# GpSimd's sums of weights, begun after the second unit of the last stage in place of the sixteenth

## The chip, the core and the metric

The kernel runs on one core of a Trainium2 chip. The core has five engines with queues of their own: TensorE (PE in the profile: matmuls, and PEld for its weight loads), VectorE (DVE), ScalarE (ACT), GpSimd (POOL) and SyncE (SP), which here only issues DMAs. GpSimd issues DMAs too, from its own queue. Sixteen DMA engines carry all of them. The metric is the device time of one execution in microseconds, the median of several runs.

## The reference

One layer of a streaming encoder over 2048 prompt frames and 32 sample frames, width 1024:

```
u = rms_norm(h);  q, k, v, a, b = split(u @ w_in)          # 8 heads of 64; conv of 512 channels
att = softmax(q k^T / 8 + rel_bias, own chunk and 8 before) v
cv  = silu(layer_norm(causal_conv31(a * sigmoid(b)) + conv_b))
h   = h + concat(att, cv) @ w_out
u   = rms_norm(h);  gate, up = split(u @ w_gate_up)         # 2 x 2816 columns
h   = h + (silu(gate) * up) @ w_down
y   = h + sigmoid(rms_norm(h) @ w_ple_gate) * (p @ w_ple_proj)
```

It also returns the newest keys, values and convolution inputs. All data is float32.

## The kernel before

The 2080 frames are five blocks of 416 columns; a product is of 128x128 weight tiles with 128x416 activations. For precision each float32 operand is split into a high part, which TensorE takes as it is, and a low part (the value less its high part); each tile product is three matmuls (high x high, high x low, low x high: `passes`, L193 to L198).

There are three stages, `project`, `attend` and `finish`. The change is in the last one. `finish` walks over a list of *units*, numbered v from 0; U0 is what the semaphore `used` counts when the stage begins, and TensorE raises it by one after each unit. A unit is one or two 128-row outputs of one weight matrix: kinds X and Y (w_out, attention half and convolution half, four units each in block 0), G and U (gate and up columns, 11 of each per half), D (w_down, 8 per half) and P (w_ple). Units 0 to 7 are X and Y of block 0, and unit 8 is its first G. The matmuls of unit 0 are issued at the end of `attend`. Most units in this stretch have 24 matmuls.

Around each unit (the numbers of buffers in brackets):

- SyncE loads the raw weights of unit v + 4 (`weights`, L2610) into one of two buffers (`x` in the trace), after the unit that held it was split. In block 0 it also stores the low parts (`low_store`, L2616) for the later blocks, which only reload them.
- ScalarE makes the high part (`high`, L2708, two buffers), VectorE the low part (`weight_low`, L2831, block 0 only, four buffers). TensorE waits for the low part.
- VectorE and ScalarE take the results out of PSUM, form squares, sigmoids and the hidden tiles (L2895 to L3024), and run the depthwise convolution of a later block in small rounds (`taps`, L2878). At the opening of the stage they also have the last steps of block 0's convolution (L2846 to L2862).

Blocks 0 to 2 are done this way. Blocks 3 and 4 are done together by `last_pair`, which saves matmuls with sums of weight tiles, as in Strassen's scheme. These sums are made by GpSimd while `finish` works on blocks 0 to 2: `weight_sums` (L1664 to L1698). It has 60 rounds (`SUMS`) with one buffer (a part of `c_top`) and no overlap between rounds: two loads of 256 KB (L1687), four additions and subtractions of 128x256 (L1689 to L1695), one store of 512 KB to the scratch tensor `w_gu_sums` (L1698). Each round waits for the store before it, and for the count `sums_after` of `used`. In `last_pair` ScalarE waits once for the last store (L1971), ahead of its fourth piece of weights (L1651), and SyncE waits for the rounds of a piece that reads them (L1876). GpSimd's only later work is L2268.

Of the kernel before, what the change touches and what calls it, by code (L numbers as in the profile page):

```python
# [17 lines left out]
KD = D // P  # L18
# [6 lines left out]
KF = FF // P  # L25
# [16 lines left out]
SINGLE, FIRST, SECOND = 3, 4, 3  # L42
# [5 lines left out]
def build(nc, t):  # L48
# [3 lines left out]
    with ExitStack() as ctx:  # L52
# [36 lines left out]
        with ExitStack() as middle:  # L89
            c["rstd"] = sb("rstd", [P, NB, N], until=middle)  # L90
            for n in ("q_in0", "q_in1", "q_in2", "q_in3", *(f"kv_in{g}" for g in range(8)), "first_g", "bias_in0", "first_z"):
# [4 lines left out]
            attend(nc, t, c, s, {"w_in": each, "hi_done": QKV + 6, "lo_done": QKV + 6, "used": NB * QKV + 4})  # L96
        GLUS = 8 * (NB - 1) + 2
        finish(nc, t, c, s, {"w_in": each + 16 * GLUS // 2, "hi_done": QKV + 6 + GLUS, "lo_done": QKV + 14,
                             "used": NB * QKV + 6 + GLUS, "low_dma": [16 * GLUS // 2] * 2 + [0] * 2})

# [2309 lines left out]
def finish(nc, t, c, s, base):  # L2410
# [6 lines left out]
    NTAP = CT * TAPS  # L2417
# [21 lines left out]
    at, count, newest, turn = {}, 0, {}, 0  # L2439
# [42 lines left out]
    with ExitStack() as ctx:  # L2482
        def sem(name):
            return ctx.enter_context(nc.semaphore("c_" + name))
# [27 lines left out]
        W0, H0, L0, U0 = base["w_in"], base["hi_done"], base["lo_done"], base["used"]  # L2512
# [9 lines left out]
        tap = sem("tap")  # L2522
# [54 lines left out]
        def late(u):  # L2577
# [10 lines left out]
            "raw": [top[:, 16 * N + e * KH * P:16 * N + (e + 1) * KH * P] for e in range(3)],  # L2588
            "hi": [flat[:, e * KH * P:(e + 1) * KH * P] for e in range(4)],
            "lo": [flat[:, (4 + e) * KH * P:(5 + e) * KH * P] for e in range(4)],  # L2590
            "newest": newest, "left0": count, "sig0": SINGLE * (KF + KD), "tap": tap, "taps": 4 * NTAP, "sums_after": U0 + 16,
            "mix_staged": MIX0 + 32,
            "pa_at": {down_b + r: k for k, r in enumerate((4, 5, 7, 8, 10, 11, 13, 14))},
            "left": left, "sig_out": sig_out, "gs_out": gs_out, "hid_out": hid_out, "hid_hi": hid_hi, "hid_lo": hid_lo,
# [612 lines left out]
```

## Time and profile before

| | |
|---|---|
| median of 3 runs | 2627.03 us (2625.26 to 2628.12) |
| profiled execution, its own time | 2624.12 us |
| its span | 2622.3 us |
| TensorE busy | 2602.2 us, 99%, 14408 matmuls |
| VectorE busy | 1803.4 us, 69% |
| ScalarE busy | 1222.0 us, 47% |
| GpSimd busy | 467.1 us, 18% |
| DMA | 675.05 MB, mean 257 GB/s |

Matmuls are pipelined: a matmul's modelled time is longer than the distance between the starts of two of them, so that short waits don't show as idle time and the number of matmuls in a stretch says more. A line of the profile names a source line of the kernel, engine and operation, what is written and read, and how long. Idle time before an instruction is put down to what ended it.

### The profile page before, as it was taken

To read this page: it belongs to the slowest core of one execution; us is meant where nothing else is said; L and a number is where in the kernel's file an instruction comes from. 1 tells how busy PE (TensorE), PEld (TensorE's weight loads), DVE (VectorE), ACT (ScalarE), POOL (GpSimd) and SP (SyncE) were. 2 spreads that over 40 slices of the span, in tenths; PEclk is the share of its full clock that TensorE was granted. 3 is DMA by queue.
4 is the path that set the end of the run, shared out by engine and by line. 5 is a ranking of instruction groups with operands and counts; after the bars stand their busy time and mean duration, and the time that the engine had idled before them with its cause. 6 is when DMAs were issued, how large, how long until landed. Compare 5 with 4: busy or idle time off the path is not lost.

```text
span 2622.3 us, 40458 instructions
## 1 busy us (share of the span) xinstructions
PE 2602.2 (99%) x14408; PEld 2542.2 (97%) x14408; DVE 1803.4 (69%) x3303; ACT 1222.0 (47%) x2240; POOL 467.1 (18%) x513
## 2 busy tenths in 40 slices
PE   9999999999999999999999999999999999999999
PEld 8999999999999999999999999999998999999999
DVE  4555478988978878777756876888548655665462
ACT  5444367877764323443334443323435443443453
POOL 6222200000001323223323323333300000000000
PEclk9999999999999999999999999999999999999999
DMA  5666798888677998898888898889895554555677
GB/s 202 213 219 233 252 356 272 266 279 267 205 236 245 296 305 281 294 345 291 319 310 313 283 322 302 318 312 317 299 317 165 169 169 153 174 162 167 196 240 236
DMA packets 316115, 675.05 MB, mean 257 GB/s; under 512 B 36589, under 2 KB 172653, under 8 KB 315373
## 3 DMA queue, kind: packets, MB, share of 16 engines
q1 hardware_dynamic: 297676, 609.55, 70.0%
q0 software_dynamic: 18240, 62.93, 6.8%
q8 instruction: 116, 1.90, 0.3%
q14 instruction: 83, 0.67, 0.1%
HBM read 514.28 MB, written 160.10 MB: 257 GB/s over the span
## 4 chain that ended last, share of the span: by engine, by line
PE 86%; DVE 7%; DMA 4%; issue 2%; ACT 2%; SPq 0%; DVEq 0%; ACTq 0%
PE psum L198 53%; PE psum L2285 23%; PE psum L1509 3%; PE psum L1485 2%; DMA x<-in_w_gu 2%; DVE y L2878 1%; PE psum L1473 1%; PE psum L1472 1%; DVE wres L2831 1%; ACT wres L2708 1%; DMA o_y<-c_top 0%; DVE wres L2087 0%; DVE plain L2078 0%; DMA a_cr<-in_cache 0%; PE psum L837 0%
## 5 line engine op out<-in xcount | busy, mean ns | idle before, releaser
L198 PE MATMUL psum<-uh,wres 128*128 128x416 f32 x3936 | 1118.2, 355 | 5.7 <-DVE wres L2831 2.4
L198 PEld LDWEIGHTS psum<-uh,wres 128*128 128x128 f32 x3936 | 736.6, 188 | 19.2 <-DVE wres L2831 5.3
L198 PE MATMUL psum<-ul,wres 128*128 128x416 f32 x1968 | 687.7, 349 | 0.0
L2708 ACT ACTIVATE wres<-x 128x1024 fp32r<-128x1024 f32 (+2 forms) x234 | 268.5, 1148 | 641.2 <-PE psum L198 533.1
L198 PE MATMUL psum<-wres 128*128 128x416 f32 x2304 | 447.7, 352 | 1.9 <-DVE wres L2831 1.6
L198 PEld LDWEIGHTS psum<-wres 128*128 128x128 f32 x2304 | 430.3, 188 | 9.3 <-issue 2.4
L2285 PE MATMUL psum<-wres 128*128 128x416 f32 x2056 | 418.7, 352 | 4.3 <-issue 1.4
L2285 PEld LDWEIGHTS psum<-wres 128*128 128x128 f32 x2056 | 383.2, 188 | 13.8 <-issue 5.6
L198 PEld LDWEIGHTS psum<-ul,wres 128*128 128x128 f32 x1968 | 370.3, 188 | 6.5 <-issue 1.4
L2878 DVE SCALAR_TENSOR_TENSOR y<-c_top,vec,y 128x416 f32<-128x416 f32 (+1 forms) x600 | 340.2, 634 | 0.8
L1651 ACT ACTIVATE wres<-c_top 128x512 fp32r<-128x512 f32 (+1 forms) x306 | 184.0, 603 | 190.1 <-PE psum L2285 48.2
L1687 POOL DMA_DIRECT2D c_top<-in_w_gu x88 | 62.3, 713 | 746.5 <-PE psum L198 517.4
L2285 PE MATMUL psum<-uh,wres 128*128 128x416 f32 x480 | 137.8, 352 | 0.0
L2285 PE MATMUL psum<-c_hx,wres 128*128 128x416 f32 x640 | 137.5, 351 | 0.2 <-ACT wres L1651 0.2
L1368 ACT ACTIVATE wres<-psum 128x384 fp32r<-128x384 f32 (+5 forms) x256 | 91.0, 405 | 89.3 <-PE psum L1485 88.8
L1239 DVE TENSOR_TENSOR wres<-psum,wres 128x384 fp32r<-128x384 f32 (+5 forms) x256 | 111.0, 441 | 16.7 <-ACT wres L1368 16.5
L2285 PEld LDWEIGHTS psum<-c_hx,wres 128*128 128x128 f32 x640 | 119.5, 188 | 2.2 <-ACT wres L1651 0.5
L2831 DVE TENSOR_TENSOR wres<-x,wres 128x1024 fp32r<-128x1024 f32 (+2 forms) x74 | 99.8, 1348 | 27.5 <-ACT wres L2708 27.5
L1689 POOL TENSOR_TENSOR c_top<-c_top 128x256 f32<-128x256 f32 x60 | 51.2, 853 | 341.4 <-DMA c_top<-in_w_gu 264.7
L1358 ACT ACTIVATE b_pr<-b_pr,b_nmx 128x640 f32<-128x640 f32 (+5 forms) x136 | 103.5, 761 | 4.1 <-DVE b_nmx L1218 4.1
L1509 PE MATMUL psum<-wres 128*128 128x256 f32 (+1 forms) x672 | 98.9, 280 | 0.0
L2285 PEld LDWEIGHTS psum<-uh,wres 128*128 128x128 f32 x480 | 89.7, 188 | 0.8 <-issue 0.2
(277 smaller groups left out, 3448.5 us busy)
## 6 DMA issues: line engine op xcount, KB each, us to landing
x<-in_w_gu SPq DMA_DIRECT2D x132, 512.0 KB, 5.4
wres<-w_gu_lo SPq DMA_DIRECT2D x88, 512.0 KB, 6.2
x<-in_w_down SPq DMA_DIRECT2D x48, 704.0 KB, 5.9
w_gu_sums<-c_top POOLq DMA_DIRECT2D x60, 512.0 KB, 6.0
c_top<-w_gu_sums SPq DMA_DIRECT2D x120, 256.0 KB, 3.0
w_gu_lo<-wres SPq DMA_DIRECT2D x44, 512.0 KB, 6.5
c_top<-in_w_gu POOLq DMA_DIRECT2D x88, 256.0 KB, 5.9
wres<-w_down_lo SPq DMA_DIRECT2D x32, 704.0 KB, 7.0
```

The costliest lines, as they stand in the source:

```text
L198: mm = nc.tensor.matmul(out, w[wp](kw), u[up](ku), start=first and n == 0 and j == 0, stop=last and n == len(kts) - 1 and j == 2)
L1239: last = nc.vector.tensor_tensor(dst(ptl), src, dst(pth).bitcast(F32), ALU.subtract)
L1358: nc.scalar.activation(pr[0:mq, q, 0:w], pr[0:mq, q, 0:w], ACT.Exp, scale=-1.0, bias=nmx[0:mq, q:q + 1], accum_out=rsum[0:mq, q:q + 1]).th ...
L1368: last = nc.scalar.activation(dst(pth), src, ACT.Copy)
L1485: mm = nc.tensor.transpose(ps_t[0:wd, part, at * P:at * P + mq], pr[0:mq, i % 3, k * P:k * P + wd], c["ident"][0:mq, 0:mq])
L1509: mm = nc.tensor.matmul(ps_o[:, q, q0:q0 + nq], rows, pt[0:wd, q, a, q0:q0 + nq], start=x == 0 and j == 0, stop=x == count - 1 and j == 1)
L1651: nc.scalar.activation(f["hi"][n % 4][:, cols], f["raw"][q][:, cols], ACT.Copy).then_inc(c["hi_done"], 1)
L1687: nc.gpsimd.dma_start(v[:, 2 * x:2 * x + 2, :], src).then_inc(moved, 16)
L2285: mm = nc.tensor.matmul(out, w[wp](k), r[rp], start=first and k == 0 and wp == rp == 0, stop=last and k == len(rights) - 1 and wp == 1, sk ...
L2708: nc.scalar.activation(whi[v % 2][:, 0:kts, :], raw[v % 2][:, 0:kts, :], ACT.Copy).then_inc(hi_done, 1)
L2831: nc.vector.tensor_tensor(wlo[v % 4][:, 0:kts, :], raw[v % 2][:, 0:kts, :], whi[v % 2][:, 0:kts, :].bitcast(F32), ALU.subtract).then_inc(l ...
L2878: last = nc.vector.scalar_tensor_tensor(y[:, ct, to], gw[:, ct, fro], vec[:, w:w + 1], y[:, ct, to], ALU.mult, ALU.add)
```

## The change

GpSimd's rounds wait for the end of unit 1 instead of unit 15. What is summed, the order, the buffer and every wait between rounds stay.

```diff
--- before.py
+++ after.py
@@ -2588,7 +2588,7 @@
-            "newest": newest, "left0": count, "sig0": SINGLE * (KF + KD), "tap": tap, "taps": 4 * NTAP, "sums_after": U0 + 16,
+            "newest": newest, "left0": count, "sig0": SINGLE * (KF + KD), "tap": tap, "taps": 4 * NTAP, "sums_after": U0 + 2,
```

The wait stands in `weight_sums`:

```python
        for n in range(SUMS):
            pool.wait_ge(c["used"], f["sums_after"])
            if n:
                pool.wait_ge(moved, sums_stored(n - 1))
```

## Rows read from the trace of the kernel before

**Rows 1.** The page: busy time of the engines, and 40 slices of the span.

```profile
PE 2602.2 (99%) x14408; PEld 2542.2 (97%) x14408; DVE 1803.4 (69%) x3303; ACT 1222.0 (47%) x2240; POOL 467.1 (18%) x513
...
PEclk9999999999999999999999999999999999999999
```

**Rows 2.** POOL's work in order of time and its stores as a group: start, duration, [idle before].

```profile
825.37 1.59 POOL L1687 DMA_DIRECT2D c_top<-in_w_gu  x2 [488.18 <-PE psum L198]
834.48 0.73 POOL L1689 TENSOR_TENSOR c_top<-c_top 128x256 f32<-128x256 f32 x1 [7.52 <-DMA c_top<-in_w_gu]
...
L1698 POOL DMA_DIRECT2D w_gu_sums<-c_top x60: 774/774/791, 839.3 to 1895.5; - x60
```

**Rows 3.** ACT in order of time, its first piece behind the wait for the sums.

```profile
1950.88 0.63 ACT L1651 ACTIVATE wres<-c_top 128x512 fp32r<-128x512 f32 x1 [0.49 <-DMA c_top<-in_w_out]
```

**Rows 4.** The chain that ended last, 740 to 940 us: start, duration, what.

```profile
767.86 6.17 DMA x<-in_w_out
...
775.14 1.23 DVE wres L2831
776.39 6.56 DMA x<-in_w_gu
...
811.17 127.25 PE psum L198 x672
```

**Rows 5.** PE and DVE in order of time, 750 to 812 us.

```profile
751.59 28.67 PE L198 MATMUL psum<-wres 128*128 128x416 f32 x148
...
792.40 0.46 PE L198 MATMUL psum<-uh,wres 128*128 128x416 f32 x1 [0.17 <-DVE wres L2831]
...
811.17 0.46 PE L198 MATMUL psum<-uh,wres 128*128 128x416 f32 x1 [0.35 <-DVE wres L2831]
...
772.74 1.09 DVE L2950 TENSOR_TENSOR z<-psum,z 128x416 f32<-128x416 f32 x2 [2.38 <-PE psum L198]
```

**Rows 6.** Windows: length, then busy us and count per engine, PE clock, DMA share, GB/s.

```profile
775.00:780.00 5.00, 5.00 (x28) 1.00 1.05 408
...
760.00:765.00 5.00, 5.00 (x29) 1.00 0.71 233
...
755.00:790.00 35.00, 35.00 (x185) 34.19 (x184) 28.19 (x46) 21.39 (x32) 0.00 (x0) 1.00 0.94 331
...
940.00:1042.00 102.00, 99.55 (x520) 96.37 (x518) 84.89 (x117) 32.40 (x42) 33.07 (x37) 1.00 0.87 282
1042.00:1830.00 788.00, 784.55 (x4132) 772.47 (x4133) 587.32 (x976) 303.34 (x385) 254.07 (x312) 1.00 0.89 310
1830.00:1900.00 70.00, 70.00 (x368) 68.45 (x367) 34.78 (x48) 30.04 (x40) 20.95 (x30) 1.00 0.87 299
...
785.00:811.00 26.00, 25.43 (x129) 23.47 (x128) 23.98 (x35) 14.04 (x20) 0.00 (x0) 1.00 0.69 211
```

**Rows 7.** DVE, then POOL, in order of time around POOL's first round.

```profile
825.79 0.59 DVE L2981 TENSOR_TENSOR c_top<-c_top 128x416 f32<-128x416 f32 x1
826.30 1.22 DVE L2831 TENSOR_TENSOR wres<-x,wres 128x1024 fp32r<-128x1024 f32 x1
827.43 2.33 DVE L2878 SCALAR_TENSOR_TENSOR y<-c_top,vec,y 128x416 f32<-128x416 f32 x4
...
834.85 0.81 DVE L2981 TENSOR_TENSOR c_top<-c_top 128x416 f32<-128x416 f32 x1
835.70 1.64 DVE L2831 TENSOR_TENSOR wres<-x,wres 128x1024 fp32r<-128x1024 f32 x1
837.27 3.29 DVE L2878 SCALAR_TENSOR_TENSOR y<-c_top,vec,y 128x416 f32<-128x416 f32 x4
...
836.34 1.60 POOL L1693 TENSOR_TENSOR c_top<-c_top 128x256 f32<-128x256 f32 x1
```

**Rows 8.** The chain, 940 to 1042 us: its longest load; then PE in order of time.

```profile
997.03 8.94 DMA x<-in_w_gu
...
1042.93 1.41 PE L198 MATMUL psum<-wres 128*128 128x416 f32 x6 [1.56 <-DVE wres L2831]
```

## The prediction

> **What bounds the kernel now.** I read the views from the coarse to the fine. The page comes first [rows 1]: TensorE (PE) is busy for 99% of the span and its granted clock is full in all 40 slices, VectorE (DVE) has 69%, GpSimd (POOL) 18%. So the time is PE's work plus the moments at which PE is made to wait; an edit that touches no PE instruction can only create or remove such moments. "Busy" hides small ones, since a matmul's modelled time (350 ns) is longer than the distance between two (127.25 us for 672, 0.189 us each [rows 4]), so I also count matmuls per stretch.
>
> Second, POOL's own view [rows 2]. Its sums are 60 rounds: two loads of 256 KB, four additions, one store of 512 KB. The first round's loads start at 825.37 us, after 488 us in which POOL had nothing, and the first and last store are issued at 839.3 and 1895.5: (1895.5 - 839.3)/59 = 17.9 us a round. What reads the sums comes later. ScalarE waits for all of them once, ahead of its fourth piece of weights for the last two blocks; that piece runs at 1950.88, after a wait of 0.49 us for its own load and none for the sums; the last store was issued at 1895.5 [rows 2, 3]. SyncE reads sums only after that. The end of the sums has some 50 us of slack, so ending earlier is worth nothing in itself.
>
> Third, the chain of waits between 752 and 811 us, the start of the last stage [rows 4]. Here the chain isn't PE. It goes through DVE (the convolution's tail and the low parts of the weights), then a weight load of 6.17 us, ScalarE, DVE, another weight load of 6.56 us, ScalarE, DVE again, and comes back to PE at 792.40; from 797.3 to 811.1 it is DVE and ScalarE once more. Only from 811.17 on does it read "PE, 127.25 us, 672 matmuls". PE waits there before 792.40 and 811.17 [rows 5]. The windows show how little room the stretch has [rows 6]: the DMA engines are busy 94% of 755 to 790 us, and DVE 24.0 of the 26 us from 785 to 811.
>
> **The change, part by part.** POOL waits for U0+16 before each round; now for U0+2. The later rounds had this count behind them anyway, so only the first moves. When is the second unit over? PE's row of 148 matmuls starts at 751.59; the first 12 end unit 0, the next 24 are unit 1, so at 28.67/148 = 0.194 us each U0+2 comes at 751.59 + 36 x 0.194 = 758.6 us. The sums start 825.4 - 758.6 = 66.8 us, or 66.8/17.9 = 3.7 rounds, earlier, and end at about 1830. Nothing is added or removed: 60 rounds, 180 DMAs from POOL's queue, 240 additions. POOL has no other work between, and SyncE's queue isn't passed or reordered.
>
> Step 1, **DMA traffic at the start**. Round 1 has its loads in 759 to 768 us (the first ones before took 834.48 - 825.37 = 9.1 us), its store from about 772, and round 2's loads from about 778 [rows 2]. Each of these three moves 0.52 MB; at 408 GB/s, the most that a 5 us window showed there [rows 6], that is 1.28 us of all engines, 3.9 us together. The free share of the windows 760 to 785 is 0.29 x 5 = 1.5 us and sits at 760 to 765, so 0 to 3.9 - 1.5 = 2.4 us falls on the two weight loads of the chain. Both lie on it, with 0.8 us of slack in front of PE's next unit: the low part of unit 6's weights is ready at 775.14 + 1.23 = 776.4 [rows 5] and PE comes to unit 6 at 751.59 + 132 x 0.194 = 777.2. The middle of 0 to 2.4 is 1.2 us; I take **+1.2 us** (0 to 2.4).
>
> Step 2, **additions beside DVE**. The row that shows the price is the first round of before, 834.5 to 839.0 [rows 7]. DVE's operations beside it took 0.81, 1.64 and 3.29 us; the same ones without POOL 0.59, 1.22 and 2.33 [rows 7]. That is 0.22 + 0.42 + 0.96 = 1.6 us a round. The additions of POOL's round 1 (768 to 772) meet DVE waiting for PE and a load, as it idles 2.38 us before 772.74 [rows 5]: 0. Round 2's additions (about 787) and round 3's (about 805) meet the chain where it is DVE. Part of the chain there is ScalarE, PE, and fixed gaps, so half of 1.6 us reaches PE each time: **+1.6 us** (0 to 3.2). Round 4's come at about 823, when the chain is PE again; the very first round of before, at 834 to 839, fell into the same run of PE, and it has no break there [rows 4, 7]: 0.
>
> At this point a rule of the Trainium skill can be set beside the row. The measured operations were stretched by a third, which looks like sharing. The Trainium skill ("SBUF — State Buffer", section "Who interferes with whom") says that VectorE with two inputs in SBUF contends with a GpSimd operation that reads SBUF, and that the loser is blocked outright for the whole instruction. Were every addition of a round (0.73 us undisturbed in its row) to block DVE in full, a round would cost 4 x 0.73 = 2.9 us instead of 1.6 us. The trace has 1.6 us, because POOL is the loser part of the time: its third addition there took 1.60 us [rows 7].
>
> Step 3, **what is taken away at the end**. Four rounds vanish from 1830 to 1900 us. PE has 368 matmuls in those 70 us, 0.190 us each, and no idle time [rows 6]: 0. DVE is at half load there, so the cover is large.
>
> Step 4, **the rounds between**. From 825 to 1830 POOL still does a round each 18 us, with another phase. PE's idle time there is 2.45 us in 940 to 1042 and 3.45 us in 1042 to 1830 [rows 6]; one wait of 1.56 us, at 1042.93, is the largest part [rows 8]. A new phase can remove or double such waits: 0, from -2 to +2 us.
>
> Sum: 1.2 + 1.6 + 0 + 0 = **+2.8 us**. A later PE start at 811 is never made good, since from there PE runs without a pause. The profiled execution took 2624.12 us (span 2622.3 and 1.8 us around it), so it would become 2626.9. It is 2.9 us below the median of the runs shown, 2627.03; on that median the forecast is 2629.8 us. A measurement of this kernel can tell about 0.2%, 5.3 us, from no change, so the forecast is "the same", leaning slow.
>
> **The rivals.**
>
> A, *hidden altogether*: -1 to +1 us, 2627. For it: the chain has PE waits of under a microsecond only, and weights are prepared one to two units ahead. Against: the chain passes through DMA and DVE for 40 us without PE.
>
> B, *the opening falls behind*: slower than I say. Both terms come at their upper end, with 2.9 us a round: that is what the skill's rule of full blocking would give here, in rounds 2, 3 and 4. By the rows: all of the 3.9 us of DMA and four rounds at 1.6 us = 3.9 + 6.4 = 10.3 us at most, half of it 5.2; 2632 to 2637. It decides from the point at which DVE, whose idle time is 26 - 24.0 = 2.0 us in 785 to 811 [rows 6], can no longer make up 1.6 us per round before the next one, 18 us later, so that PE waits at each unit from 792 to about 850. Against: from 811 to 938 six rounds ran beside a DVE with much the same work, and PE had no pause [rows 4].
>
> C, *faster*: the new phase clears the stretch 940 to 1042. The chain there holds weight loads of up to 8.9 us [rows 8] against 6.2 and 6.6 us at the opening [rows 4], and PE has 520 matmuls instead of 102/0.189 = 539 [rows 6]. The 19 missing ones are 3.6 us, and the PE idle of 1042 to 1830 is 3.45 us more. If most of it went and the opening cost nothing, the gain is 5 to 7 us: 2621. It needs both, and rounds stay as frequent there as before.
>
> D, *the start doesn't move*: would POOL be held by something else than the count? It has only this wait and an empty queue before it. Its effect would be that of A.
>
> **Chances.** Forecast (+1 to +5 us) 0.55; A with D 0.23; B 0.17 (0.13 of it above +5.3 us); C 0.05 (0.02 beyond -5.3 us). So faster 0.02, same 0.85, slower 0.13. Range: the forecast's own bounds are 0 and 2.4 + 3.2 = 5.6 us, and -2 to +2 for the phases and about 1.5 us for the spread of the three runs; together 2626 to 2634, which leaves out 1 in 10 on either side.
>
> **What the next profile would show.** POOL's first load at 758 to 759 us and its last store near 1829. In the opening: the weight loads of the chain above 6.6 us, DVE's 128x1024 subtraction at 1.6 us in place of 1.22 beside POOL's second and third round, and the unbroken run of PE starting 2 to 4 us after 811.2. In 1830 to 1900 the same 368 matmuls. Step 1 is wrong if those loads stay at 6.2 to 6.6 us; step 2 if PE's waits in 780 to 811 don't grow while DVE's rows do; step 3 if PE gains matmuls at the end. The prediction fails on the slow side if PE waits at each unit up to 850, on the fast side if 940 to 1042 has its full 539 matmuls.

## The result and the profile after

The change makes the kernel slower. In six runs beside six of the kernel before, the median is 2634.6 us against 2626.15 us, +8.45 us; the ratio is 1.0029, with a 95% interval of 1.0018 to 1.0039. Ten more runs of the same kernel, the experiment `e11_change_again` below, gave 1.0023 (1.0013 to 1.0033). The forecast was +2.8 us, "the same, leaning slow", with a range of 2626 to 2634 us: the sign was right and the size too small; the first measurement lies just above the range, and the +6.0 us of the second would lie inside it. The ratios, here and below, leave out three far slower executions (2852, 4279 and 6625 us), which the medians include.

The page of the changed kernel differs little from that of the kernel before [rows 1]: TensorE is busy 3.2 us longer and the span is 9.1 us longer.

```profile
PE 2605.4 (99%) x14408; PEld 2545.4 (97%) x14408; DVE 1803.3 (69%) x3303; ACT 1222.7 (46%) x2240; POOL 472.2 (18%) x513
```

2.4 of the 9.1 us lie before the changed place: the last group of matmuls ahead of the stage's stream starts at 751.52 us in this trace and at 749.12 in that of the kernel before. Over all the traces here that moment lies between 749.1 and 753.3, without any edit ahead of it. So from here on I count from the opening, T0, the first matmul of this group (L1572).

GpSimd starts as forecast, after unit 1. Its work in order of time, and its stores as a group (compare [rows 2]):

```profile
761.59 1.59 POOL L1687 DMA_DIRECT2D c_top<-in_w_gu  x2 [423.60 <-PE psum L198]
767.96 0.73 POOL L1689 TENSOR_TENSOR c_top<-c_top 128x256 f32<-128x256 f32 x1 [4.78 <-DMA c_top<-in_w_gu]
...
L1698 POOL DMA_DIRECT2D w_gu_sums<-c_top x60: 777/777/793, 772.5 to 1856.2; - x60
```

The chain that ended last, 755 to 905 us (compare [rows 4]). The two weight loads of the opening take 7.38 and 8.66 us, and the chain then stays with loads and VectorE; the long run of TensorE, from 811 us before, comes only behind 902 us.

```profile
770.62 7.38 DMA x<-in_w_out
...
780.37 8.66 DMA x<-in_w_gu
...
834.34 7.21 DMA x<-in_w_gu
...
845.99 9.37 PE psum L198 x48
...
866.99 7.91 DMA x<-in_w_gu
```

TensorE in order of time. In the kernel before there were only short waits here, 0.17 to 0.35 us [rows 5]; now there is a long one at 791.79, and there are more behind 811:

```profile
791.79 0.48 PE L198 MATMUL psum<-uh,wres 128*128 128x416 f32 x1 [2.04 <-DVE wres L2831]
...
814.86 0.45 PE L198 MATMUL psum<-uh,wres 128*128 128x416 f32 x1 [1.13 <-DVE wres L2831]
821.15 0.46 PE L198 MATMUL psum<-uh,wres 128*128 128x416 f32 x1 [1.49 <-DVE wres L2831]
...
845.99 0.46 PE L198 MATMUL psum<-uh,wres 128*128 128x416 f32 x1 [1.44 <-DVE wres L2831]
```

Behind the wait of 2.04 us TensorE's clock is at its lower level, 1.2 in place of 2.4 GHz, for some 3.4 us. The windows below (length, TensorE busy and count, granted clock, DMA share, GB/s) have a granted clock of 0.50. Their counts include matmuls that run across a window's ends; a window of 1 us at full clock counts 7. By the starts, 14 matmuls take 4.30 us from 791.79 on, where 14 x 0.189 = 2.65 us were enough: about 1.7 us are lost on top of the wait.

```profile
791.00:792.00 1.00, 0.21 (x1) 1.00 0.09 35
792.00:793.00 1.00, 1.00 (x4) 0.54 0.16 23
793.00:794.00 1.00, 1.00 (x4) 0.50 0.75 188
794.00:795.00 1.00, 1.00 (x5) 0.50 0.84 225
795.00:796.00 1.00, 1.00 (x6) 0.76 1.04 418
```

A cost of another kind: GpSimd's third round of additions meets the first step of the convolution, a tensor_scalar of VectorE with one large input. Its four take 3.46 us; in the kernel before they took 1.71 us. GpSimd isn't slowed at all there. VectorE in order of time in the kernel before, then VectorE and GpSimd after:

```profile
800.79 1.71 DVE L2888 TENSOR_SCALAR y<-c_top,vec 128x416 f32<-128x416 f32 x4
```

```profile
809.01 3.46 DVE L2888 TENSOR_SCALAR y<-c_top,vec 128x416 f32<-128x416 f32 x4
...
809.02 0.73 POOL L1689 TENSOR_TENSOR c_top<-c_top 128x256 f32<-128x256 f32 x1 [8.18 <-DMA c_top<-in_w_gu]
809.82 0.76 POOL L1691 TENSOR_TENSOR c_top<-c_top 128x256 f32<-128x256 f32 x1
```

The windows that answer to [rows 6]: the loss is in the opening. 785 to 811 us has 111 matmuls instead of 129, and 1830 to 1900 has the same 368. In between, 940 to 1830 us has 30 matmuls more than before, of which more below.

```profile
755.00:790.00 35.00, 34.02 (x178) 32.66 (x176) 25.76 (x36) 17.21 (x25) 8.63 (x11) 1.00 0.98 350
785.00:811.00 26.00, 23.54 (x111) 21.37 (x110) 20.74 (x26) 14.48 (x19) 8.03 (x10) 0.93 0.76 259
940.00:1042.00 102.00, 100.70 (x531) 98.69 (x530) 86.13 (x118) 31.34 (x39) 33.46 (x36) 1.00 0.89 290
1042.00:1830.00 788.00, 787.26 (x4151) 775.96 (x4150) 586.77 (x977) 303.02 (x386) 245.48 (x302) 1.00 0.88 310
1830.00:1900.00 70.00, 70.00 (x368) 68.46 (x367) 35.77 (x51) 31.19 (x41) 9.02 (x12) 1.00 0.73 259
```

### The profile page after: what moved, and what is told of

It is laid out like the page before. It is cut to its first block, busy times and chain, and to the rows that moved or that the text cites. A ratio compares the mean times of both kernels' runs of the same rounds, so it can differ in the third digit from the quotient of the medians.

```text
span 2631.4 us, 40458 instructions
## 1 busy us (share of the span) xinstructions
PE 2605.4 (99%) x14408; PEld 2545.4 (97%) x14408; DVE 1803.3 (69%) x3303; ACT 1222.7 (46%) x2240; POOL 472.2 (18%) x513
## 4 chain that ended last, share of the span: by engine, by line
PE 86%; DVE 6%; DMA 4%; issue 2%; ACT 1%; SPq 0%; POOL 0%; DVEq 0%; ACTq 0%; POOLq 0%
PE psum L198 53%; PE psum L2285 23%; PE psum L1509 3%; PE psum L1485 2%; DMA x<-in_w_gu 2%; PE psum L1473 1%; DVE wres L2831 1%; PE psum L1472 1%; DVE y L2878 1%; ACT wres L2708 1%; DMA o_y<-c_top 0%; DMA a_room<-in_w_in 0%; DVE wres L2087 0%; DMA a_cr<-in_cache 0%; PE psum L837 0%
```

## The experiments

One number is read from each trace: TensorE's matmuls in the 140 us behind T0, up to about 889 us, where block 0's first D unit begins. These are the windows of the kernel before, its second profile (`e8`), the change, and its second profile (`e11`), in this order:

```profile
749.12:889.12 140.00, 139.25 (x723) 1.00 0.85 274
```

```profile
749.53:889.53 140.00, 137.88 (x713) 1.00 0.83 269
```

```profile
751.52:891.52 140.00, 132.05 (x667) 0.99 0.85 285
```

```profile
750.93:890.93 140.00, 135.64 (x691) 0.99 0.86 287
```

At 0.189 us each, the change is 56 and 32 matmuls behind the first trace, a *lag* of 10.6 and 6.1 us, and the kernel before differs from itself by 10, or 1.9 us. One trace is good to some 2 to 4 us. The totals of the two measurements, +8.45 and +6.0 us, differ by as much.

| kernel | matmuls to T0 + 140 | lag, us | median, before beside it | ratio (95%) |
|---|---|---|---|---|
| before, twice | 723, 713 | 0, 1.9 | | |
| the change | 667 | 10.6 | 2634.6, 2626.15 | 1.0029 (1.0018 to 1.0039) |
| `e11` the change again | 691 | 6.1 | 2634.02, 2628.06 | 1.0023 (1.0013 to 1.0033) |
| `e1` additions cut | 702 | 4.0 | 2628.32, 2626.7 | 1.0004 (0.9995 to 1.0013) |
| `e2` DMAs cut | 699 | 4.5 | 2629.24, 2626.7 | 1.0007 (0.9997 to 1.0017) |
| `e3` both cut | 719 | 0.8 | 2627.6, 2626.7 | 1.0001 (0.9993 to 1.001) |
| `e6` first round only | 712 | 2.1 | 2630.58, 2626.62 | 1.0021 (1.0012 to 1.003) |
| `e4` start after unit 8 | 682 | 7.8 | 2631.49, 2626.7 | 1.0018 (1.0008 to 1.0029) |
| `e12` after unit 11 | 718 | 0.9 | 2628.14, 2628.06 | 1.0006 (0.9994 to 1.0017) |
| `e5` after unit 23 | 722 | 0.2 | 2627.03, 2626.62 | 1.0004 (0.9995 to 1.0013) |
| `e7` pause | 719 | 0.8 | 2626.85, 2626.62 | 1.0008 (0.9995 to 1.0022) |
| `e9` late taps, early sums | 691 | 6.1 | 2635.22, 2628.06 | 1.0031 (1.0019 to 1.0043) |
| `e10` late taps | 721 | 0.4 | 2633.18, 2628.06 | 1.0018 (1.0006 to 1.003) |

### Which part of a round costs: traffic or additions

For `e1_tiny_adds` the first six rounds add 8 of 256 columns (w = 8, q = 256); for `e2_tiny_dmas` they move 8 of 256 columns (w = 256, q = 8), with a memset of the buffer first and the missing stores made up ahead of the last round; for `e3_both_tiny` both are 8. `sums_after` is U0 + 2, and each of the six rounds waits for four more units than the one before. This holds the shortened rounds apart, but the third starts 49 to 52 us behind T0, against 48 in the change, and the fourth 68 to 72 against 65, so the meetings with VectorE aren't exactly those of the change.

```diff
-            pool.wait_ge(c["used"], f["sums_after"])
+            pool.wait_ge(c["used"], f["sums_after"] + 4 * min(n, 5))
+            w, q = (8, 256) if n < 6 else (256, 256)
...
-                nc.gpsimd.dma_start(v[:, 2 * x:2 * x + 2, :], src).then_inc(moved, 16)
+                nc.gpsimd.dma_start(v[:, 2 * x:2 * x + 2, 0:q], src[:, :, 0:q]).then_inc(moved, 16)
...
-            nc.gpsimd.tensor_tensor(a22, a21, a22, ALU.add).then_inc(made, 1)
+            nc.gpsimd.tensor_tensor(a22[:, 0:w], a21[:, 0:w], a22[:, 0:w], ALU.add).then_inc(made, 1)
```

> The sums start after unit 1, as in the change, but in the first six rounds, from 760 to about 860 us, the four additions work on 8 of 256 columns (the sums of these rounds are not those of the reference); all DMAs keep their full size, and round n of the six waits for unit 1 + 4n. The profile of the change shows TensorE 60 matmuls (11.3 us) behind at 940 us. Theory DMA (the traffic of the rounds delays the chain's weight loads): nearly all of the cost stays, 8 us or more of the 11.3 and weight loads of 7 to 9 us at the opening. Theory additions (VectorE is slowed beside GpSimd's additions, and the chain is VectorE's): the cost falls to 3 us or less, and the loads get shorter by themselves as they start earlier. If both share it: 4 to 7 us.

> The counterpart: additions at full size, while the loads and the store of the first six rounds move 8 of 256 columns, 1/32 of the bytes (the missing stores are made up late, before the last round; the sums of these rounds are not those of the reference). Theory DMA: little cost is left at 940 us, 0 to 3 us behind the kernel before. Theory additions: 8 us or more of the 11.3 stay, with VectorE's 128x1024 subtraction at 1.6 us in the opening beside each round. If both share it: 4 to 7 us, and the two experiments add up to about the whole.

> The control: additions and DMAs of the first six rounds are both cut to 8 of 256 columns. Both theories: TensorE is not behind at 940 us (less than 1 us), and the total is that of the kernel before or some us less, since 940 to 1800 us then has the same rounds with another phase, and the last rounds end 60 us earlier. If 4 us or more remain at 940 us, the cost is in something else than bytes and additions: GpSimd's queue, its DMA issues or the semaphores.

Measured: lags of 4.0, 4.5 and 0.8 us. Neither theory holds alone; the cost is shared. With both cut the lag is within the spread of the kernel before, so the queue, the issue of the DMAs and the semaphores cost nothing that shows. 4.0 - 0.8 = 3.2 us are the traffic's alone and 4.5 - 0.8 = 3.7 us the additions'; together with the 0.8 that is 7.7 us, between the change's two traces. Each of these is from one trace and good to some 2 us.

The rows bear the two parts out. The two weight loads of the opening's chain take 8.59 and 7.50 us in `e1` and 5.81 and 6.58 us in `e2`. In `e2` TensorE's clock halves behind a wait of 1.57 us and one of 0.23 us, which costs the same 1.7 us as above; it doesn't in `e1`. So of the 3.7 us some 1.7 are the clock's and some 2.0 are left for waits on VectorE. VectorE comes late there because GpSimd's second round (additions up to 790.2 us) meets four operations on its chain, which take 0.58 to 0.65 us each in the kernel before. VectorE in order of time in `e2_tiny_dmas`:

```profile
786.35 1.13 DVE L2904 SCALAR_TENSOR_TENSOR ul<-z,vec,uh 128x416 fp32r<-128x416 f32 x1
787.40 1.12 DVE L2910 TENSOR_TENSOR c_top<-c_top 128x416 f32<-128x416 f32 x1
788.45 1.12 DVE L2904 SCALAR_TENSOR_TENSOR ul<-z,vec,uh 128x416 fp32r<-128x416 f32 x1
789.49 1.12 DVE L2910 TENSOR_TENSOR c_top<-c_top 128x416 f32<-128x416 f32 x1
```

GpSimd's additions beside them start at 787.10, 788.15 and 789.20 us, the same 1.05 us apart: the two engines go in turns, and both are slowed (the additions take 0.97 us, 0.73 undisturbed).

In the totals the parts are +1.6 and +2.5 us and not clear of zero, while both together, the change, are. Why they don't add up there isn't shown.

### One round alone

```diff
-            pool.wait_ge(c["used"], f["sums_after"])
+            pool.wait_ge(c["used"], f["sums_after"] + 14 * (n > 0))
```

> Only the first round starts after unit 1; the other 59 wait for unit 15 as before. Theory of full DMA engines (755 to 790 us): the first round's loads and store, and its additions beside the weights of units 4 and 5, already cost 3 to 5 us at 940 us, with the chain's two weight loads at 7 us or more. Theory that it is a matter of how long the rounds go on while VectorE is behind: 0 to 1.5 us.

Measured: a lag of 2.1 us, under the 3 to 5 us expected by the one theory and above the other's 1.5. The loads on the chain did lengthen, as step 1 of the forecast has it:

```profile
770.47 7.28 DMA x<-in_w_out
...
780.12 7.60 DMA x<-in_w_gu
```

With 6.17 and 6.56 us before [rows 4] that is 2.15 us more, and 2.1 us arrive. A single load says little, since it spreads without any early round too (5.61 to 7.55 us); the sum of the two is steadier. It is 12.4 to 13.5 us in the eight traces in which both are on the chain and no full-size DMA of a round is beside them, 14.9 us here, and 16.0 to 16.6 us in the four with two rounds of full traffic (the change twice, `e1`, `e9`).

The total is +4.0 us, more than the opening explains. This trace has a wait of 2.46 us at 965 us, and the clock halves behind it; from T0 + 190 to T0 + 290 it has 497 matmuls where the kernel before has 514 and 516, some 3 us. The chain isn't TensorE's there in the kernel before either. Whether the first round has to do with it stays open.

### From which unit on the sums are free

`e4_start9`, `e12_start12` and `e5_start24` are the kernel before with `"sums_after": U0 + 9`, `U0 + 12` and `U0 + 24`.

> The sums start after unit 8 (about 791 us) in place of unit 1 or 15, nothing else changed. Theory DMA (the full DMA engines of 755 to 790 us): most of the cost is avoided, 0 to 3 us behind at 940 us, since only VectorE is full from here on. Theory additions: the rounds still meet VectorE at over 90% in 785 to 820 us, so 4 to 8 us of cost.

> The sums start after unit 11 (about 805 us). Start after unit 8 cost 8.1 us at 140 us after the opening and 4.8 us in total, start after unit 15 nothing. Theory reserve: VectorE makes up its backlog between 791 and 825 us, so the price falls in between, 2 to 5 us at 140 us and 1.5 to 4 us in total. Rival (the price is that of a few coincidences of a round with a critical operation): anything from 0 to 8 us, not in order of the start.

> The sums start after unit 23 (about 861 us), 36 us later than in the kernel before; the last round would end near 1936 us, still ahead of ScalarE's wait near 1950. Theory (the opening's G and U units up to 889 us can't carry rounds because VectorE and the weight loads have no reserve there): in the kernel before, the two rounds at 825 to 861 us fell into a run of TensorE with no break, so nothing or at most 1 us is gained at 940 us. Total: the kernel before, within 2 us. Rival (each round in that stretch costs 2 us or more wherever it falls): 3 to 5 us faster. If the slack at the end was misread: slower, with ScalarE waiting for the sums at 1950 us.

Measured: after unit 8 a lag of 7.8 us, nearly the change's, though its first loads start at 795 us, behind the stretch of full DMA engines. After unit 11 0.9 us, within the spread, and nothing more to gain after unit 23. The price doesn't fall slowly with the start, as the theory of reserve had it for `e12` (2 to 5 us); it stops between units 8 and 11. The chain of `e4_start9` shows what its rounds met:

```profile
804.83 2.98 DVE y L2888 x4
...
820.14 1.77 DVE wres L2831
...
830.17 8.40 DMA x<-in_w_gu
...
841.19 1.76 DVE wres L2831
```

These are the tensor_scalars of the convolution again (2.98 against 1.71 us), two weight subtractions of 1.77 in place of 1.22 us, and a load of 8.40 us. TensorE waits 2.62 us behind the last, and its clock halves again:

```profile
843.00 0.46 PE L198 MATMUL psum<-uh,wres 128*128 128x416 f32 x1 [2.62 <-DVE wres L2831]
```

In `e12_start12` the first load comes behind the tensor_scalars, which keep their 1.71 us. VectorE, then GpSimd:

```profile
803.15 1.71 DVE L2888 TENSOR_SCALAR y<-c_top,vec 128x416 f32<-128x416 f32 x4
...
808.96 1.59 POOL L1687 DMA_DIRECT2D c_top<-in_w_gu  x2 [469.95 <-PE psum L198]
```

The split is the same in the other traces: 2.98 to 3.46 us where full-size additions meet them (the change twice, `e2`, `e4`, `e9`), 1.71 us elsewhere.

`e5_start24` also measures the slack at the end. Its last store is issued at 1946.3 us and ScalarE waits 5.1 us for it:

```profile
ACT wres L1651 <- DMA w_gu_sums<-c_top: 5.1, 1, 5.1
```

In the trace read for the prediction the last store is at 1895.5, so its slack is 1946.3 - 5.1 - 1895.5 = 46 us, near the 50 us read there. That isn't a property of the kernel alone. In the second trace of the kernel before (`e8`) the stores as a group are

```profile
L1698 POOL DMA_DIRECT2D w_gu_sums<-c_top x60: 777/777/793, 839.0 to 1924.7; - x60
```

and leave some 16 us.

### A pause in the second half

```diff
-            pool.wait_ge(c["used"], f["sums_after"])
+            pool.wait_ge(c["used"], f["sums_after"] + 35 * (n >= 7))
```

> The kernel before with a pause: round 7 (959 us in the kernel before) and all after it wait for unit 50 (about 1000 us), so that 959 to 1000 us has no round; the end moves to about 1936 us. TensorE lost 19 matmuls (3.6 us) in 940 to 1042 us in the kernel before, with two or three rounds in the paused part. Theory (rounds cause these waits): 1.5 to 3 us are gained by 1042 us, and the total is 1 to 3 us lower. Rival (the convolution's taps and the weight loads cause them by themselves, or the change's own traces, which lost only half as much there with as many rounds, just had another phase): 0, within 1 us either way.

Measured: 2626.85 against 2626.62 us, ratio 1.0008 (0.9995 to 1.0022). No gain in the total. In the trace, T0 + 190 to T0 + 290 has 529 matmuls where the kernel before has 514 and 516, so 2.5 to 2.8 us are gained in the paused part, as the theory had it; the 50 us ahead of it, with a wait of 1.61 us at 894 us, have ten fewer than the first trace of the kernel before, which takes most of it back. But `e1`, `e4` and `e12` have 523 to 525 there without a pause. What the rounds cost in that stretch isn't settled.

### Is it VectorE's reserve

`e10_late_taps` moves convolution rounds out of the first half's U units, `e9_late_taps_early_sums` does so with U0 + 2.

```diff
-            1: spread(60, places("U", 0) + places("D", 0) + places("U", 0, 1)),
+            1: spread(60, places("D", 0) + places("U", 0, 1)),
```

> The change, and with it the 60 convolution rounds for block 1 are spread over the D units and the second half's U units alone, none over the first half's U units. That takes 2.3 us of VectorE's work out of each pair of G and U units from 800 to 889 us. The change's trace is 10.8 us behind at 140 us after the stage opened (889 us), the kernel before 0 and 1.7 us in its two traces. Theory reserve (after the opening VectorE has nearly no idle time, so that each round's 1.6 us and its later weight loads reach TensorE): the lag at 140 us falls to 3 to 6 us, what the first two rounds and the clock cost. Theory of the weight loads (rounds lengthen them, and the ring of two buffers is too short, whatever VectorE does): it stays at 8 us or more. The total isn't comparable with the kernel before, as the second half gets more work; it is with the next kernel.

> The control of the one before: the convolution rounds moved, the sums after unit 15 as before. Both theories: 0 at 140 us after the opening, within 1 us, since TensorE had no wait there but at the opening; behind by some us at 310 us, where the second half now has three convolution rounds per unit. The total 0 to 10 us above the kernel before. The difference of the two totals is the price of the early start when VectorE has more idle time: 3 to 5 us by the theory of reserve, 8 us by the other.

Measured: 6.1 and 0.4 us of lag. All of `e9`'s waits in the 140 us stand ahead of 797 us, the largest 1.74 us and the next 1.56 with the clock halved behind them; the next one, 1.16 us, comes at 896 us, with rounds 17 to 19 us apart in between. That agrees with reserve. But `e11_change_again`, with the convolution rounds in place, has its last wait of the 140 us at 823.59 and the same lag of 6.1 us. Against that trace nothing was gained, so the experiment doesn't decide. The difference of the totals is 2635.22 - 2633.18 = 2.0 us, less than the change's own 6 to 8, with intervals that overlap.

### The same kernels again

> The kernel before, profiled a second time, to see what two traces of one kernel differ by: the time at which the last stage opens (749 to 753 us in the traces so far), TensorE's count of matmuls at 940 us after the opening (both theories: equal within 1 us), and the count in 940 to 1042 and in the two later places (1580 to 1620, 1740 to 1780 us) where the change's trace gained back 5 us. If this trace also gains there, the 5 us are no effect of the change.

> The change itself a second time. It says how far one trace may be trusted: the lag at 140 us after the opening was 10.8 us. If TensorE's clock falls again after a wait of 2 us or more at the first G unit, that is a part of the change's price; if not, it is an accident of one trace. Total: 7 to 9 us above the kernel before.

Measured: the second trace of the kernel before has one wait more in the 140 us, 1.01 us at 881.5, and 0.79 us at 891.6. So the unbroken run of TensorE from 811 to 938 us was in part luck of the first trace. The second settles another point. The change's first trace seemed to win back some 5 us late, between 940 and 1100 us and around 1600 and 1750 us. In 1560 to 1630 and 1730 to 1800 the first trace of the kernel before has 360 and 365 matmuls, its second one has

```profile
1560.00:1630.00 70.00, 70.00 (x366) 1.00 0.86 300
1730.00:1800.00 70.00, 70.00 (x373) 1.00 0.91 324
```

so those waits were an accident of the trace read for the prediction, and the change gives nothing back there. Over the whole way from T0 + 140 to T0 + 1850 something may come back: its two traces have 8953 and 8949 matmuls, the kernel before 8933 and 8936, which is 2.5 to 3.8 us, and the eight other kernels that leave the convolution rounds in place have 8913 to 8938. The totals, +8.45 and +6.0 us, don't show it.

The change's second trace repeats the opening: loads of 7.24 and 8.78 us, a wait of 2.06 us at the first G unit, and the clock halved behind it.

## Why the prediction fell short, by its steps

**Where the time goes** was right. The loss arises behind T0 and ahead of the first D unit, and 1830 to 1900 us has its 368 matmuls (step 3, 0 us, right). Step 4 took 0 for the rounds between, from -2 to +2 us; the change's traces seem to get 2.5 to 3.8 us back there, if that is more than spread. The start was right within a microsecond once the trace's own 2.4 us are taken off. The last store came at 1856 and not 1829, because a round took 18.4 us and not 17.9; it took 18.4 us in the second trace of the kernel before as well and 18.1 in that of the change, so this is spread and not the change's doing, and it costs nothing.

**Step 1, traffic**, is the term that was most too small. The mechanism was right, with both weight loads on the chain. I took the middle of 0 to 2.4 us, 1.2, by counting free DMA capacity. The two loads together grew by 1.21 + 2.10 = 3.3 us in the change (3.1 us against the mean, 12.9 us, of the eight traces without early traffic), by 2.15 us in `e6` with one round, and the traffic alone cost 3.2 us in `e1`. The bound was wrong as well: bytes at the highest rate, set against the free share, gave at most 2.4 us. Why a load grows by more than that no run shows. The later loads of the change's chain (7.21 and 7.91 us) don't count against it: the second trace of the kernel before has 6.74 and 8.28 us at 846 and 865 us.

**Step 2, additions**: 1.6 us (0 to 3.2) against 3.7 us in `e2`, 2.0 without the clock. So the size was nearly right, and where it arises in part wrong. "Round 1: 0" was wrong: its additions stretch VectorE's work ahead of the first load (in the change the subtraction at 769.01 takes 1.59 us), and TensorE waits 0.51 us at 769.35 in `e2`. "Half reaches TensorE" was too little at round 3: in `e2` the tensor_scalars take 3.41 us, 1.7 more, and the two waits of TensorE behind them are 0.30 and 1.48 us against 0.35 us before, so 1.4 of the 1.7 us arrive. The price was read beside operations with two inputs, and the tensor_scalars lose as much alone, 1.75 us in the change. "Round 4: 0" nearly held: the wait of 1.49 us at 821.15 ends ahead of round 4's first addition at 822.82, and the wait behind that round is 0.17 us (0.18 in `e11`). The 1.44 us at 846 us come behind round 5 and a load of 7.21 us, and only in the first of the change's traces.

**What no step had** is the clock: 1.7 us more behind a wait of about 2 us at the first G unit, in both traces of the change. In `e2` and `e9` it falls near the same place, behind a wait of under 1.6 us with one of 0.23 us close by, in `e4` at 843 us behind 2.62 us, and in the opening of no other kernel here. With 3.2 us of traffic, 2.0 of additions, 1.7 of the clock and the 0.8 that `e3` leaves, the sum is 7.7 us, where the forecast had 1.2 + 1.6 = 2.8.

**The rivals.** B, the opening falls behind, had the price that was measured (2632 to 2637). Its sign, a wait at each unit from 792 to about 850 us, came only in part: the change's first trace has five waits of over 0.2 us there, in some twelve units, and its second trace has two. I gave B 0.17, against it the run of 811 to 938 us; that argument was weak, as the second trace of the kernel before shows. Whether its mechanism, VectorE's missing reserve, is the cause `e9` couldn't decide. The Trainium skill's rule of full blocking ("SBUF — State Buffer", section "Who interferes with whom") stood behind the same rival with 2.9 us a round. The traces have less: single operations grew by up to 0.58 us (the subtraction from 1.22 to 1.59 or 1.77 us, additions from 0.58 to 1.12 or 1.16 us), less than one undisturbed addition of 0.73 us each, and the largest price of a round read here is the 2.0 us by which the four operations of `e2` grew. A, C and D are out: the cost is clear of zero, nothing was faster, and GpSimd did start early.

What stays open: why the cost ends between a start after unit 8 and after unit 11. VectorE's backlog and a chance meeting of rounds with the tensor_scalars and one load both fit; `e9` couldn't part them. No version tried beats the kernel before.

## What to carry to other kernels

Work put under another engine's cover is as cheap as the stretch it is moved into, not as it was where it ran: before moving it, read whose chain that stretch is, and if it is the engine or the queue that the work shares, count the price at each meeting, from the first one on, and look whether a wait grows long enough for TensorE's clock to fall behind it. Background work whose end has 16 to 46 us of slack has nothing to gain from an earlier start; let it wait until the main engine is the chain. When two traces of one kernel differ by 2 us at the place of interest, profile both kernels twice before reading gains of that size.

## What the runs showed of the hardware

- Single waits of TensorE of 2.04 us (the change), 2.06 (`e11`), 2.46 (`e6`) and 2.62 us (`e4`) were each followed by some 3.4 us at half clock. Single waits of 1.44 and 1.49 us (the change), 1.56 us (the kernel before, [rows 8]), 1.62 (`e1`) and 1.80 us (`e10`, at 1046.5 us) were not. In `e2` two waits of 1.57 and 0.23 us close together were, and in `e9` two of 1.56 and 0.23 us.
- VectorE's tensor_scalar of 128x416, one tensor as input and factors per partition, went from 0.43 to 0.87 us each beside GpSimd's additions, which kept their 0.73 to 0.76 us (the change). Operations with two tensors as inputs went from 1.22 up to 1.77 us (128x1024) and from 0.58 up to 1.16 us (128x416), and slowed GpSimd too (0.73 to 1.60 us).
- Two weight loads of 512 KB one after the other took 12.4 to 13.5 us together in eight traces, and 16.0 to 16.6 us in four with two load pairs and a store of 0.5 MB each from GpSimd's queue among them.
- Two traces of one kernel, the kernel before, differed by 10 matmuls in 140 us and by 29 us in the time of GpSimd's last store.
